# The odd mixer of a hybrid decoder trunk: the latents' norm behind their projections, and two heads in flight on three PSUM banks each

## The reference

```python
def mla_mixer(h, positions, w_down, q_norm_w, w_uq, kv_norm_w, w_ukv, w_o):
    # 8 heads, q rank 384, kv rank 256, 128 + 64 (rotary) columns a head, values of 128
    cq, ckv, k_rope = jnp.split(h @ w_down, [MLA_Q_RANK, MLA_Q_RANK + MLA_KV_RANK], axis=-1)
    q = (rmsnorm(cq, q_norm_w) @ w_uq).reshape(b_, t, MLA_HEADS, MLA_QK)
    q_nope, q_rope = q[..., :MLA_NOPE], q[..., MLA_NOPE:]
    kv = (rmsnorm(ckv, kv_norm_w) @ w_ukv).reshape(b_, t, MLA_HEADS, MLA_NOPE + MLA_V)
    k_nope, v = kv[..., :MLA_NOPE], kv[..., MLA_NOPE:]
    q_rope = apply_rope(q_rope, cos[:, :, None, :], sin[:, :, None, :])
    k_rope = apply_rope(k_rope, cos, sin)
    for start in range(0, t, ATTN_BLOCK):      # blocks of 128 queries
        s = (einsum(q_nope, k_nope[:, :end]) + einsum(q_rope, k_rope[:, :end])) * MLA_QK ** -0.5
        p = softmax(where(mask, s, -inf))
        outs.append(einsum(p, v[:, :end]))
    return concatenate(outs) @ w_o
```

## Time and profile before

| | before |
|---|---|
| median of 3 runs | 2294.81 us (2293.04 to 2295.93) |
| the profiled execution | 2296.76 us, span 2295.0 us |
| TensorE busy (share of the span) | 2209.9 us (96%) |
| VectorE, ScalarE, GpSimd busy | 916.9, 766.5, 74.3 us |
| granted TensorE clock, mean | 0.98 |
| HBM read | 193.60 MB |
| odd mixer: latent tile 4 to the start of the out projection | 1684.26 to 1881.44 us |

### The profile page before, as it was taken

One profiled execution on the slowest core, in us unless ns is written; L12 is line 12 of the kernel. 1 busy time (PEld: TensorE's weight loads), 2 busy tenths in 40 slices (PEclk: granted clock), 3 DMA queues, 4 the chain that ended last, 5 costly groups with the idle time before them and its releaser, 6 DMA issues.

```text
span 2295.0 us, 25279 instructions
## 1 busy us (share of the span) xinstructions
PE 2209.9 (96%) x10542; PEld 1821.5 (79%) x10542; DVE 916.9 (40%) x1312; ACT 766.5 (33%) x1204; POOL 74.3 (3%) x79
## 2 busy tenths in 40 slices
PE   6999999999998899999999999999998889999999
PEld 6888888778777788988888888888875358888887
DVE  4333324565645543533322533332454335333322
ACT  4322223433445543422222332222233344222221
POOL 0000000000000000000000000000033000000000
PEclk9999999999999999999999999999998799999999
DMA  5233322211111113323333233233222002333331
GB/s 186 92 102 101 101 92 72 92 56 56 47 56 55 56 56 129 111 92 94 105 96 100 94 100 103 99 101 92 65 89 88 0 28 80 104 99 103 100 93 55
DMA packets 55298, 197.35 MB, mean 86 GB/s; under 512 B 6144, under 2 KB 6784, under 8 KB 55184
## 3 DMA queue, kind: packets, MB, share of 16 engines
q1 hardware_dynamic: 53856, 193.75, 26.4%
q10 hardware_dynamic: 1328, 1.97, 0.2%
HBM read 193.60 MB, written 2.10 MB: 85 GB/s over the span
## 4 chain that ended last, share of the span: by engine, by line
PE 86%; DVE 6%; ACT 5%; issue 2%; DMA 0%; POOL 0%; SPq 0%; DVEq 0%; ACTq 0%
PE ps L941 16%; PE ps L942 16%; PE ps L943 16%; PE ps L949 9%; PE ps L950 9%; PE ps L951 9%; PE ps L1395 1%; PE ps L1394 1%; DVE w_lo L1456 1%; PE ps L1105 1%; DVE a_rows L1462 1%; PE ps L1107 1%; PE ps L1106 1%; PE ps L1181 1%; PE ps L1218 1%
## 5 line engine op out<-in xcount | busy, mean ns | idle before, releaser
L941 PE MATMUL ps<-h_hi,w_hi 128*128 128x512 f32 (+1 forms) x1848 | 686.5, 372 | 6.1 <-ACT a_rows L635 3.2
L943 PE MATMUL ps<-h_hi,w_lo 128*128 128x512 f32 (+1 forms) x1848 | 680.8, 368 | 0.0
L942 PE MATMUL ps<-h_lo,w_hi 128*128 128x512 f32 (+1 forms) x1848 | 680.6, 368 | 0.0
L478 ACT ACTIVATE w_hi<-raw 128x1024 fp32r<-128x1024 f32 x352 | 370.4, 1056 | 719.1 <-PE ps L943 363.6
L1456 DVE TENSOR_TENSOR w_lo<-raw,w_hi 128x1024 fp32r<-128x1024 f32 x337 | 403.0, 1221 | 373.8 <-ACT w_hi L478 373.1
L941 PEld LDWEIGHTS ps<-h_hi,w_hi 128*128 128x128 f32 x1848 | 350.2, 190 | 68.1 <-ACT a_rows L635 3.9
L943 PEld LDWEIGHTS ps<-h_hi,w_lo 128*128 128x128 f32 x1848 | 350.0, 189 | 57.5
L942 PEld LDWEIGHTS ps<-h_lo,w_hi 128*128 128x128 f32 x1848 | 350.4, 190 | 56.4
L1456 DVE TENSOR_TENSOR a_rows<-a_rows,ps 128x512 f32<-128x512 f32 x88 | 60.6, 688 | 613.5 <-PE ps L943 613.5
L949 PE MATMUL ps<-w_hi,a_hi 128*128 128x512 f32 x704 | 274.4, 390 | 0.0
L951 PE MATMUL ps<-w_hi,a_lo 128*128 128x512 f32 x704 | 273.9, 389 | 0.0
(11 more groups left out here) (199 smaller groups left out, 1950.9 us busy)
## 6 DMA issues: line engine op xcount, KB each, us to landing
raw<-in_w_gate_up SPq DMA_DIRECT2D x176, 512.0 KB, 3.8
raw<-in_w_down SPq DMA_DIRECT2D x88, 512.0 KB, 3.6
raw<-in_w_vg SPq DMA_DIRECT2D x16, 512.0 KB, 3.6
raw<-in_w_xbc SPq DMA_DIRECT2D x16, 512.0 KB, 3.6
raw<-in_w_even_out SPq DMA_DIRECT2D x16, 512.0 KB, 3.7
raw<-in_w_qk_small SPq DMA_DIRECT2D x9, 512.0 KB, 3.6
raw<-in_w_z SPq DMA_DIRECT2D x8, 512.0 KB, 3.6
raw<-in_w_odd_out SPq DMA_DIRECT2D x8, 512.0 KB, 3.5
```

Of the source, the lines that this page charges most:

```text
L478: return nc.scalar.activation(to, source, ACT.Copy, scale=scale)
L941: nc.tensor.matmul(to, w_h, hi, start=first, stop=False)
L942: nc.tensor.matmul(to, w_h, lo, start=False, stop=False)
L943: return nc.tensor.matmul(to, w_l, hi, start=False, stop=last)
```

## The change

Only the odd mixer changes, with the weight slots that it loads.

- The latents come in another order: two of K/V, the rotary key, three of Q. They are not copied out. ScalarE squares them in PSUM and takes the high part with the gain as scale, VectorE the low part with one operation. The row norm is left out there. For K it is multiplied in when VectorE takes a tile out of PSUM (`take_k`), for V as ScalarE's scale (`take_v`), and for Q it is part of the scale of the exponential (`score_scale`), so a K/V norm has to be spread and a Q norm not.
- VectorE makes both tables of angles during the latents, and the loads that they need are issued earlier in ScalarE's queue (inside `boundary`).
- The weights of Q, K and V are one stage `up` of 9 slots (before: 5, of which one was a half, 2 and 2), in the order in which `plan_odd` uses them: K and Q of the first pair of heads, all V, then Q and K of the pairs 1 to 3.
- Scores of a head take three banks, in three groups (query tile 3; tiles 2 and 0; tile 1). Even heads use banks 2 to 4, odd ones 5 to 7, for scores, turned probabilities and output. Projections use banks 0 and 1 meanwhile. After the scores of head n come the Q or K projections of the next pair (n below 6), then the values of head n-1. The copies of Q and V rows are gone.
- The first slot of the out projection goes between the scores and the values of head 7.
- The float32 matmuls of a head, the 204 fp32r matmuls of the projections and those of the latents and the out projection stay the same in number and shape.

```diff
+def plan_odd():
+    kinds = [("k", 0), ("q", 0), ("v", 0), ("v", 1)] + [(kind, i) for i in range(1, MH // 2) for kind in ("q", "k")]
+    banks = [4, 5, 6, 7, 0, 1, 4, 5, 6, 7, 0, 1, 5] + 3 * [0, 1, 0, 0, 1]
...
+        SCORE_GROUPS = (((3, 0, 0),), ((2, 0, 1), (0, 3 * P, 2)), ((1, 0, 3),))
+        SCORE_BANKS = ((2, 3, 4), (5, 6, 7))
...
                 if b == ODD:
                     split_some("latent", INNER, 6)
...
+                    split_some("up", 0, 1)
+                    power(norms["kv_latent"], rstd_col[:, :])
+                    split_some("up", 1, 5)
+                    power(norms["q_latent"], rstd_q)
+                    split_some("up", 5, 9)
                     split_some("odd_out", 0, INNER)
```

ScalarE:

```diff
+                for n in range(6):
+                    take_latent(n)
+                    split_high(first + INNER + n)
+                    if n in (1, 4):
+                        row = sin if n == 1 else cos
+                        act.wait_ge(angle_ready, 1 if n == 1 else 2)
+                        nc.scalar.activation(row, row, ACT.Sin).then_inc(table_ready, 1)
+                act.wait_ge(latent_lo_ready, QR + KR)
+                square_latent(5)
+                take_q(2)
+                take_q(3)
+                split_high(up_first + 4)
...
+                for n in range(MH):
+                    exponentials(n)
+                    if n % 2 == 0 and n < MH - 2:
+                        for m in range(3):
+                            take_q(13 + 5 * (n // 2) + m)
+                    if n:
+                        values_of(n - 1)
+                    if n == 0 or 2 <= n < 6:
+                        split_high(up_first + 8 + max(n - 1, 0))
+                values_of(MH - 1)
```

TensorE:

```diff
                 first_four(s)
+                norm_sums(0, latent_squares[0], 2, range(NC))
+                latent(4)
+                pe.wait_ge(diag_ready, 1)
+                nc.tensor.matmul(ps[:, 3, :], ones[:, :], other[1], start=True, stop=True).then_inc(spread_ready, 1)
+                latent(5)
+                tile(0)
+                tile(1)
+                pe.wait_ge(mean_ready, norms["kv_latent"] + 1)
+                turn(0, 2)
+                for u in (2, 3, 4):
+                    tile(u)
+                pe.wait_ge(rstd_ready, 1)
+                norm_sums(1, latent_squares[2], 3, (3, 2, 0, 1))
+                tile(5)
+                turn(1, 2)
+                for u in range(6, 13):
+                    tile(u)
+                for n in range(MH):
+                    scores_of(n)
+                    if n < MH - 2:
+                        u = 13 + 5 * (n // 2)
+                        if n % 2 == 0:
+                            for m in range(3):
+                                tile(u + m)
+                        else:
+                            turn(n // 2 + 2, 1)
+                            tile(u + 3)
+                            tile(u + 4)
                     if n:
...
+                        values_of(n - 1)
...
+                halves = first_half(s, block_source, lambda k: pe.wait_ge(o_lo_ready, k + 1))
+                for _ in range(2 * NC):
+                    next(halves)
+                values_of(MH - 1)
+                for _ in halves:
+                    pass
+                second_half(s, block_source)
```

VectorE:

```diff
+                dve.wait_ge(odd_in, 48)
+                after(nc.vector.tensor_copy(angle[1], angle[0].bitcast(I32)))
+                after(ts(angle[0], angle[1], inv_freq, None, ALU.mult))
+                angles(0.0, sin)
+                latent_low(0)
+                latent_low(1)
+                sum_squares((0, 1))
+                mean_square(0, 2, KR * P)
+                latent_low(3)
+                dve.wait_ge(rstd_col_ready, norms["kv_latent"] + 1)
...
+                angles(0.25, cos)
+                latent_low(4)
+                dve.wait_ge(spread_ready, 1)
+                nc.vector.tensor_copy(rstd_rows, ps[:, 3, :]).then_inc(rstd_ready, 1)
+                latent_low(5)
+                dve.wait_ge(rstd_ready, 1)
+                take_k(0)
+                take_k(1)
+                rotate(0, 2)
+                sum_squares((2, 3, 4))
+                rotate(1, 2)
+                mean_square(1, 3, QR * P)
...
+                for n in range(MH):
+                    maxima(n)
+                    if n % 2 and n < MH - 2:
+                        rotate(n // 2 + 2, 1)
+                    normalise(n)
+                    if n % 2 and n < MH - 2:
+                        take_k(16 + 5 * (n // 2))
+                        take_k(17 + 5 * (n // 2))
+                    if n:
+                        output_low(n - 1)
+                output_low(MH - 1)
```

More of the change, by code:

```diff
@@ L349, in build_trunk @@
         o_hi_ready, o_lo_ready = sem("o_hi_ready"), sem("o_lo_ready")
-        q_up_done = sem("q_up_done")
         block = ctx.enter_context(nc.Block())
[L355 to L362, removed]
+        odd_tiles, up_end = plan_odd()
+        up_first = stages["up"][0]
+        tile_signals, tiles_inside = [], 0
+        for kind, _, m, at, _ in odd_tiles:
+            end = at + {"k": KR, "q": QR, "v": KR * NC}[kind] - 1
+            if end == up_end[end // 8] and (kind != "v" or m == NC - 1):
+                tile_signals.append((slot_done, up_first + end // 8 + 1))
+            else:
+                tiles_inside += 1
+                tile_signals.append((up_done, tiles_inside))
         FAR = [(0, 1), (1, 2), (2, 3), (0, 2), (1, 3), (0, 3)]
@@ L837, in odd @@
-                ahead = first + INNER + 6
-                for i in range(MH // 2):
-                    if i < MH // 2 - 1:
-                        act.wait_ge(q_up_done, i + 1)
-                    else:
-                        act.wait_ge(slot_done, stages["k_up"][0])
-                    for m, row in enumerate((QN + 2 * i, QN + 2 * i + 1, QROPE + i)):
-                        copy(rows(a_rows, row), ps[:, 3 * (i % 2) + m, :]).then_inc(q_taken, 1)
-                    split_high(ahead + i)
@@ L1064, in ffn @@
                              lambda k: pe.wait_ge(a_lo_ready, FT * f + k + 1))
-            def projection(name, start, stop):
-                first = stages[name][0]
-                for n in range(start, stop):
-                    slot_ready(first + n)
-                    for k in range(DK):
-                        last = products(first_bank(n), first + n, k * P, h_hi[:, k, :], h_lo[:, k, :], k == 0, k == DK - 1)
-                    last.then_inc(slot_done, 1)
             def even():
@@ new lines, in odd, with latent, norm_sums @@
+                free = {4: (latent_lo_ready, 1), 5: (latent_lo_ready, 2), 6: (krope_taken, 1), 7: (latent_lo_ready, 3),
+                        0: (latent_lo_ready, 4), 1: (latent_square, QR + KR)}
+                def latent(n):
+                    slot_ready(first + n)
+                    for k in range(DK):
+                        last = products(first_bank(n), first + n, k * P, h_hi[:, k, :], h_lo[:, k, :], k == 0, k == DK - 1)
+                    last.then_inc(slot_done, 1)
+                def norm_sums(n, source, bank, chunks):
+                    pe.wait_ge(latent_summed, n + 1)
+                    for column, c in enumerate(chunks):
+                        last = nc.tensor.matmul(ps[:, bank, column:column + 1], source[:, c * P:c * P + P], ones[:, 0:1], start=True, stop=True)
+                    last.then_inc(sums_ready, 1)
@@ L1994, in odd, with take_k @@
-                maxima(0, 0)
-                for i in range(MH // 2 - 1):
-                    pair(i, False)
-                pair(MH // 2 - 1, True)
-                out_stage(s, last_slot[s] + INNER)
+                    tt(source if j else krope, other[0], other[1], ALU.add).then_inc(rope_done, 1)
+                def take_k(u):
+                    kind, i, m, block, bank = odd_tiles[u]
+                    dve.wait_ge(*tile_signals[u])
+                    tt(rows(a_rows, KN + 2 * i + m), ps[:, bank, :], rstd_rows, ALU.mult).then_inc(k_taken, 1)
```

529 lines of the change are left out of this document (232 added, 297 removed).

## The result

| | before | after |
|---|---|---|
| median, same chip | 2295.37 us (4 runs) | 2246.69 us (4 runs, 2242.85 to 2250.04) |
| ratio | | 0.9773 (95%: 0.9755 to 0.9791) |
| profiled execution, span | 2296.76, 2295.0 us | 2246.73, 2244.8 us |
| TensorE busy | 2209.9 us | 2187.1 us |
| mean granted clock | 0.98 | 0.99 |

The kernel is 2.3% faster, at 0.7 us from the forecast of 2246. The busy line of the page after answers to the earlier trace rows: TensorE's busy time fell by 22.8 us, less than half of the gain, and the other engines' did not move.

What follows compares the result with a forecast made beforehand. TensorE's own path was taken as the bound (busy 2209.9 of 2295.0 us). Replacing 197.2 us by 35.9 plus 110.7 gains 50.5: from the 2294.81 median 2244.3, plus 1.7 for the clock, 2246 us; range 2240 to 2262.

Steps and rivals of the forecast that it cites:

- Until the first scores: From latent tile 4 to head 0's scores: 35.9 us of TensorE work, so scores start at 1720.2 instead of 1770.10.
- bounds for the tables: VectorE's second angle table, beside GpSimd's splits, could delay the three Q tiles by 0 to 3 us; taken as 0.
- The heads: From the first scores to the out projection: scores, projections, transposes and values 108.8 us, plus 1.9 of waits, total 110.7.
- the prediction's last paragraph: Signs of being right or wrong; among them, a pair of heads with projections takes about 29 us.
- the price of the four products: Value products of one head in float32 at 2.4 GHz, priced at 2.32 us within 3.96 us for transposes and values.
- K copies: In heads 1, 3 and 5, VectorE's long list could expose 0 to 1 us each before the next scores; taken as 0.
- values of n-1 behind the scores of n give the softmax its time: Heads: softmax may take until after the next scores and previous values; 3.9 or 6.2 us of projections cover heads 0 to 5.
- 0.4 of a fall of 4.2: Gaps of heads 6 and 7 may cost one clock fall of 4.2 us, chance about 0.4, so 1.7 us added.
- The list of falls before: Clock falls in the old odd mixer: after standstills of 3.4 and 5.4 us, and after 1.36 us in head 4.
- The first rival: Clock falls four to six times in the heads, at 4.2 us each: 17 to 25 us back, 2262 to 2270; chance 0.14.
- The second rival: Late copies or K tiles stop interleaving in the heads; only 20 us gained, about 2271; chance 0.08.
- The slower rival: Clock lost at the first scores and never back: +109 us against the 50.5 gain, about 2353; chance 0.03.

Runs made afterwards that it cites:

- e6: Kernel after, with the first out projection slot split into three pieces among the scores of heads 6 and 7 and the last values; 2242.25 us, ratio 0.9761.
- e3: Kernel after, with one head in flight: values of a head directly behind its scores and the following projections; 2251.45 us, ratio 0.9800.
- e2: Kernel after, with all Q and K projections and rotary products ahead of the first scores, two heads still in flight; 2260.87 us, ratio 0.9838.
- e5: Kernel after, with six extra ScalarE copies that make TensorE wait before head 0's scores; 2256.47 us, ratio 0.9819.
- e8: e2 with seven ScalarE copies as a gap before the first scores, no projections among the heads; 2278.24 us (one run).
- e0: The kernel after, unchanged, run and profiled once more; 2243.23 us, ratio 0.9762.
- e7: e6 with a Q or K tile, or an out projection piece, between a head's eighth and ninth transpose; 2238.65 us, ratio 0.9741.

## Why the prediction was right

**Until the first scores.** 1687.45 to 1722.63 is 35.2 us; the sum said 35.9. Its bounds for the tables (0 to 3 us) and the small loads (0 to 1) came out at 0, as taken. The tables' estimate of 6.8 us for the second was 6.1, and the last low part was 3.3 us early.

**The heads.** From 1722.63 to the corresponding start of the out projection (1836.74 less the 5.55 us of the slot done early, 1831.19) are 108.6 us; the sum said 110.7. A pair with projections takes 29.08 us (1747.89 to 1776.97), as the prediction's last paragraph said, though the terms of its sum give 29.7. The values are the term that was too large: 1744.17 to 1747.89 is 3.72 us, not 3.96, and eight times 0.24 are 1.9. The wait for ScalarE's first copy was sized rightly (0.25 us, against 0.23 in the sum). What was wrong is the price of the four products: I took the row's 2.32 us, but its end overlaps the next row, and from start to start it is 2.16 (1745.73 to 1747.89). The scores took 5.78 instead of 5.85. Behind the scores of heads 6 and 7 the transposes (of heads 5 and 6) wait 1.50 us each, so 1.25 more than elsewhere, where I added 0.95: 0.6 too little in all. K copies, for which I took 0 of 0 to 1 us three times, exposed nothing.

**The waits.** That nothing covers the scores of heads 6 and 7 was right, and e6 shows its price: 2.3 us. The step "values of n-1 behind the scores of n give the softmax its time" is right but small while projections are there (e3, 5.4 us); the projections do more (e2, 17.7), and only both gone cost 40.0.

**The clock.** No fall in the odd mixer, where I allowed 1.7 us (0.4 of a fall of 4.2). That the clock is a large part of the gain is what the earlier trace rows said, and the window of 0.85 against 1.00 shows it to be half. The list of falls before was short by two: the clock also fell during the 4.33 us for K's banks, ahead of 1743.08, and during the 3.35 us ahead of 1875.21. The sum didn't need them, since it is made of prices at 2.4 GHz. The first rival, that scores with half their rows pull it down again and again in the heads, did not happen, even with the 1.50 us waits; e2, where one such wait did cost a fall, shows that it wasn't far. The length of a short wait alone doesn't decide: in the kernel before, a wait of 1.36 us ahead of 1824.35 went with a fall, and one of 1.36 us ahead of 1850.87 didn't. The second rival (no interleaving, 20 us gained) didn't happen either. The slower rival is refuted by e5 and e8, where a gap made the clock low at the first scores: it came back, at a price of 6.6 and 11.6 us.

**The rule on transposes.** The prediction weighed that transposes don't count as a busy TensorE (the Trainium skill, TensorE: Matmul & The Clock Gate, "Part 4: PE-mode transpose") against the row at 1795.65. e8 is the cleaner case: 21.8 us of scores left the clock at 0.50, then came the transposes from 1785.77 and some 0.6 us of value products, and the clock was back. By the rule those 0.6 us alone must have done it. For these float32 transposes the measurement speaks against the rule, but it isn't the last word: no run has transposes with no value products behind them.

**What cancelled.** My gain for the stretch was 50.5 (less 1.7 for the clock), the traces show 53.4. The forecast itself stood on the median of 2294.81 (2244.3 plus 1.7); on the profiled execution, from which the rows are, the same sum gives 2248. The 3.2 us by which the even mixer ran later in the profiled execution brought the total back to the forecast: 0.7 us of error is luck, 3 to 5 us is what the working was good for. e0, the same kernel, had a median 3.5 us lower.

**Still open.** Why the even mixer's clock falls at other places in each execution; nothing here was changed to tell. Why a wait of 1.3 to 2.1 us goes with a fall in one place and not in another. And e7's 1.2 us beyond its waits.

## What to carry to other kernels

Give TensorE work that needs nothing from the softmax (the next heads' projections, a piece of the next product) at each place where it would wait, and cost a gap at its length plus the low clock behind it: here 27 us of waits took some 25 us of clock with them. Counted over the odd mixers of all eleven traces (1688 to 1890), each of the 18 gaps of 3.3 us or more that TensorE met at full clock went with a fall, in it or within 2.1 us behind it; of the 30 gaps of 1.3 to 2.1 us, 8 did. So a long gap cost clock every time here, and a short one about one time in four. Test two edits that cover the same wait apart and together, since alone each looks cheap (5.4 and 17.7 us, but 40.0 together). Compare a local change by the time from a fixed instruction to the end of the span when something ahead of it varies: it repeated to 0.1 us here, in two traces, where the whole repeats to 3 us or worse.

## What the hardware showed beyond that

**Work that keeps the clock doesn't have to be work that lifts it.** In the kernel after, scores run at 1.00; behind a gap, 21.8 us of the same scores stay at 0.50 (e8), until transposes and values follow; in e5 10.7 us of them stay there until fp32r projections follow.

**VectorE doesn't run slower beside GpSimd, it stands still.** I took the 2.87 us for the diagonals for a slower rate. In the kernel after, two of GpSimd's splits, and VectorE beside the second of them:

```profile
1690.12 2.39 POOL L452 TENSOR_TENSOR w_lo<-raw,w_hi 128x1024 fp32r<-128x1024 f32 x1
...
1724.61 2.34 POOL L452 TENSOR_TENSOR w_lo<-raw,w_hi 128x1024 fp32r<-128x1024 f32 x1 [3.05 <-ACT w_hi L500]
```
```profile
1725.15 0.69 DVE L1968 TENSOR_REDUCE mixer_cols<-ps 128x1 f32<-128x512 f32 x1
1725.88 1.09 DVE L1491 SCALAR_TENSOR_TENSOR mixer_cols<-mixer_cols 128x1 f32<-128x1 f32 x1
```

The maxima, read from PSUM, take their usual 0.69 us. The next operation, on one column, takes 1.09 us and ends at 1726.97, with the split (1726.95). The diagonals at 1690.19 end at 1693.06, 0.55 behind the split's 1692.51. The same one-column operation ends within 0.02 us of the split's end in five more heads of this trace. An operation that starts shortly ahead of a split keeps its usual time: in e2 0.68 us for one at 1738.02, ahead of the split at 1738.18. So it is the start of the VectorE operation within the split that sets its cost, not its length, and it depends on where it reads. This agrees with the Trainium skill, SBUF — State Buffer, section "Who interferes with whom": the two engines share a port pair, and where VectorE needs it (for a second input from SBUF, or in a two-port mode) the engine that issues first holds it for its whole instruction while the other is blocked. In e2 the same thing held up a rotation (2.75 us at 1726.64 and at 1738.74, both ending 0.55 behind a split) and the K copies behind it, and made TensorE's two waits of 2.1 and 2.0 us; with the second came a fall of the clock.
